# Attention over two key blocks in place of three with guards, a weight ring of 16 slots, and the first MLP products of two passes in seven-product form

## The chip, the cores and the metric

The kernel is one program that runs on all 8 cores of a Trainium2 chip, each core on two of the 16 sequences; the cores exchange nothing. The metric is the device time of the slowest core in microseconds. Engines are named PE (TensorE), DVE (VectorE), ACT (ScalarE), POOL (GpSimd) and SP (SyncE).

## The reference

```python
# x (16, 2048, 1024) float32; two layers; four MLP quarters of 1024 hidden columns each
for layer in range(2):
    xn = rmsnorm(h, mix_norm_g[layer])
    if layer == 0:
        p = xn @ ab_w_in                              # 2048 columns
        a_out = pool_mixer(p[:512]); b_out = gate_b * short_conv(gate_c * xb)
        mix = concat([a_out, b_out]) @ ab_w_out
    else:
        p = xn @ cd_w_in                              # 2560 columns: u, v, q, k, value
        c_out = spatial_gating(gelu(u), gelu(v))      # within 128-position chunks
        d_out = stick_breaking_attention(q, k, v)     # 8 heads of 64
        mix = concat([c_out, d_out]) @ cd_w_out
    h = h + mix
    hn = rmsnorm(h, mlp_norm_g[layer])
    h = h + square(relu(hn @ mlp_w1[layer])) @ mlp_w2[layer]
return rmsnorm(h, final_norm_g)

# attention: weight of key s for query t > s
#   A[t, s] = sigmoid(z_ts) * prod_{s<j<t} (1 - sigmoid(z_tj)),   z = q.k / 8
```

The reference sums over all earlier keys. The product in A falls fast with distance, so that only near keys count in float32.

## The kernel before

Each core holds its two sequences (s=0, 1) transposed, channels on partitions, and works through them in two halves of 1024 positions (p=0, 1), each half in two tiles (t=0, 1) of 512 positions. The residual stream `h` is float32 in on-chip memory; `xn` (normed input), `mix` and `hid` (hidden values of one MLP quarter) are bf16. A weight block of 128 output columns by 1024 inputs fills two slots of `ring` (12 slots, 6 blocks in flight). In p=0 the blocks come as float32 from `wblk` and are cast on the way, and SP stores them as bf16 in `wsc`, from where later passes load them.

`program` writes the stages in turn and weaves main work with side work: layer 0's input and mixers (`layer0_in`), `out_proj`, `mlp(s, l)` for layer l, layer 1's input (`layer1_in`), and `attention(s, p)`, which lies beside an MLP of the other sequence. The order on each engine is then set by a planner (`Sched.order`): from entered durations it works out a latest time for every operation and lists them by it, engine by engine. Every change of a duration or of the work therefore replans all stages.

The MLP has four quarters. A first product (`up`) is 8 matmuls of 128x128 weights by 512 columns for each of 8 blocks and 2 tiles; ACT applies Relu in the bank and Square into `hid`. The second product (`pairs`) adds to `h` on DVE. Where the sums of a pair of weight blocks exist in `wcm`, it runs in seven-product form (`strassen`): a group of two blocks by two tiles by two halves of the inputs takes 7 products of 4 matmuls, 28 in place of 32, with sums of the moving operand made by DVE (`tsum`). `combos` makes the weight sums (4 element-wise operations on 128x512) the first time that the blocks pass, on DVE for layer 0 and on POOL for layer 1, and SP stores them. `up_strassen` is the same form for the first product: it stands in the code but is called by nobody, since no call of `mlp` has `alone` or `mk` set.

The attention handles one unit for each of 4 pairs of heads, 16 query blocks of 128 and 2 sequences, 128 units in all. A unit scores its queries against the query's own block and the two before it (PE, L2134, two heads side by side in the rows of the array), ACT makes keep = sigmoid(-z/8), a DVE scan multiplies from the right (C, L2143), DVE subtracts neighbours (A), SP transposes A by DMA into AT, and PE multiplies with V (L2177, two heads side by side in the columns). POOL copies the leftmost product of each row to `flags`. If at the end one of them is over 0, a general kernel over all keys runs behind the first one.

## Time and profile before

| | |
|---|---|
| three runs | 2658.72, 2695.6, 3011.68 us; median 2695.6 |
| profiled execution | 2660.62 us, spans of the cores 2643.1 to 2659.0 |
| TensorE busy, slowest core | 2559.8 us (96%) |
| VectorE, ScalarE, GpSimd busy | 1555.2, 1119.1, 685.5 us |
| mean granted TensorE clock, by core | 0.991 to 0.994 |

The first row is what the comparison rests on; the others are of one execution and its slowest core, core 7. The chain that ended last goes through TensorE for 87% of the span. A line such as L1384 or L1397 is that of a helper that all stages use, so the tiles tell which stage a row belongs to: ps<-xn is a product from the normed input, ps<-hid and ps<-TT the second MLP product in seven-product form.

### The profile page before, as it was taken

Reading aid. Unit: us, or ns where it says so; the run is one execution under the profiler, and the core shown is the slowest. Engines: PE = TensorE matmul, PEld = TensorE weight load, DVE = VectorE, ACT = ScalarE, POOL = GpSimd, SP = SyncE. Lnnn points to the kernel's source line nnn. Section 1 sums busy time; section 2 is a strip of 40 time slices with the busy share of each in tenths; the row PEclk is TensorE's granted clock in tenths of the full one; section 3 lists DMA queues with packets and bytes.
Section 4 is the critical chain, followed back from the end, with each engine's and each line's share of the span. In section 5 each row is a group of like instructions: output and inputs, shape, how many; then the busy total and the mean of one; then the engine's idle time right before and its main releaser. Section 6 shows DMA issues by size and latency. Waiting matters only on the chain.

```text
span 2659.0 us, 38510 instructions; the slowest of 8 cores (2643.1 to 2659.0 us)
## 1 busy us (share of the span) xinstructions
PE 2559.8 (96%) x12392; PEld 1125.4 (42%) x12392; DVE 1555.2 (58%) x2133; ACT 1119.1 (42%) x1685; POOL 685.5 (26%) x1081
## 2 busy tenths in 40 slices
PE   5899999999999999999999999999999999999996
PEld 1344444444444444444444444444444443444443
DVE  2771337468674775436476533667776588854435
ACT  3335223464334642264333444236442364345432
POOL 2531111222112353621245211212322122311111
PEclk9999999999999999999999999999999999999998
DMA  6677884746454996855472233423564236533534
GB/s 137 152 151 159 185 188 114 160 109 140 125 125 109 166 199 131 206 159 168 124 223 79 72 101 102 135 72 93 129 136 131 76 85 133 117 103 111 161 113 148
DMA packets 237627, 354.05 MB, mean 133 GB/s; under 512 B 121072, under 2 KB 126576, under 8 KB 237424
## 3 DMA queue, kind: packets, MB, share of 16 engines
q0 software_dynamic: 77952, 227.92, 36.8%
q1 hardware_dynamic: 158896, 122.54, 18.0%
q8 instruction: 108, 1.77, 0.3%
q10 hardware_dynamic: 576, 1.05, 0.1%
q14 instruction: 95, 0.78, 0.1%
HBM read 298.26 MB, written 79.69 MB: 142 GB/s over the span
## 4 chain that ended last, share of the span: by engine, by line
PE 87%; DMA 4%; issue 3%; DVE 3%; POOL 2%; ACT 1%; SPq 0%; DVEq 0%; POOLq 0%; ACTq 0%
PE ps L1384 65%; PE ps L1498 19%; DMA ring<-wblk 2%; PE ps L2177 1%; PE ps L2134 1%; DMA ring<-wcm 1%; DMA h<-xT 1%; DVE xn L1400 1%; POOL X L1397 1%; POOL TT L1397 1%; ACT ps L1393 1%; DMA AT<-A 1%; DVE h L1397 0%; PE ps L2052 0%; SPq L1681 0%
## 5 line engine op out<-in xcount | busy, mean ns | idle before, releaser
L1384 PE MATMUL ps<-xn,ring 128*128 128x512 bf16 x5872 | 1312.0, 381 | 29.5 <-ACT XB L1393 7.7
L1384 PEld LDWEIGHTS ps<-xn,ring 128*128 128x128 bf16 x5872 | 564.9, 98 | 716.2 <-issue 60.2
L1397 DVE TENSOR_TENSOR h<-ps,h 128x512 f32<-128x512 f32 x816 | 552.3, 687 | 526.2 <-PE ps L1498 348.0
L1393 ACT ACTIVATE ps<-ps 128x512 f32<-128x512 f32 x632 | 366.7, 583 | 677.8 <-PE ps L1384 353.0
L1322 POOL DMA_DIRECT2D ring<-wsc x364 | 196.5, 540 | 733.1 <-PE ps L1384 483.3
L1498 PE MATMUL ps<-hid,ring 128*128 128x512 bf16 x1408 | 331.5, 380 | 9.5 <-DMA ring<-wcm 4.8
L1393 ACT ACTIVATE hid<-ps 128x512 bf16<-128x512 f32 x512 | 304.3, 598 | 40.2 <-ACT ps L1393 1.8
L1393 ACT ACTIVATE xn<-h 128x2048 bf16<-128x2048 f32 (+1 forms) x92 | 152.9, 1682 | 364.8 <-DVE h L1397 344.2
L1384 PE MATMUL ps<-hid,ring 128*128 128x512 bf16 x1280 | 281.2, 379 | 0.0
L1322 POOL DMA_DIRECT2D ring<-wcm x214 | 114.5, 536 | 574.6 <-PE ps L1384 283.4
L1498 PE MATMUL ps<-TT,ring 128*128 128x512 bf16 x1056 | 255.8, 380 | 5.7 <-ACT ps L1393 3.5
L1400 DVE SCALAR_TENSOR_TENSOR xn<-h,cfs,ms 128x512 bf16<-128x512 f32 x256 | 199.4, 824 | 87.7 <-ACT ms L1393 87.7
L1384 PE MATMUL ps<-mix,ring 128*128 128x512 bf16 x1024 | 227.0, 382 | 0.0
L1498 PEld LDWEIGHTS ps<-hid,ring 128*128 128x128 bf16 x1408 | 133.4, 98 | 176.8 <-issue 23.3
L2143 DVE TENSOR_TENSOR_SCAN C<-keep,cbs 128x768 f32<-128x768 f32 x112 | 198.4, 1773 | 13.7 <-DVE A L1397 4.8
L1322 POOL DMA_DIRECT2D ring<-wblk x188 | 101.2, 539 | 405.5 <-PE ps L1384 328.7
L1384 PEld LDWEIGHTS ps<-hid,ring 128*128 128x128 bf16 x1280 | 123.8, 98 | 149.1 <-issue 0.9
L1498 PEld LDWEIGHTS ps<-TT,ring 128*128 128x128 bf16 x1056 | 98.4, 98 | 138.0 <-issue 28.3
L1384 PEld LDWEIGHTS ps<-mix,ring 128*128 128x128 bf16 x1024 | 100.5, 98 | 122.6 <-issue 4.0
L1393 ACT ACTIVATE keep<-ps 128x768 f32<-128x768 f32 (+2 forms) x128 | 98.4, 769 | 80.6 <-DVE C L2143 51.9
L1397 DVE TENSOR_TENSOR A<-C 128x766 bf16<-128x766 f32 (+2 forms) x128 | 120.8, 944 | 17.6 <-DMA AT<-A 16.7
L1384 PE MATMUL ps<-ring,xn 128*128 128x512 bf16 x512 | 112.8, 379 | 1.0 <-DVE vnb L1405 0.8
(85 smaller groups left out, 1311.3 us busy)
## 6 DMA issues: line engine op xcount, KB each, us to landing
ring<-wsc POOLq DMA_DIRECT2D x364, 256.0 KB, 3.1
ring<-wblk POOLq DMA_DIRECT2D x188, 256.0 KB, 5.7
ring<-wcm POOLq DMA_DIRECT2D x66, 512.0 KB, 4.1
ring<-wcm POOLq DMA_DIRECT2D x88, 384.0 KB, 3.8
wsc<-ring SPq DMA_DIRECT2D x124, 256.0 KB, 4.3
h<-xT SPq DMA_DIRECT2D x64, 256.0 KB, 7.2
wcm<-TT SPq DMA_DIRECT2D x64, 256.0 KB, 5.1
oT<-stg SPq DMA_DIRECT2D x56, 256.0 KB, 4.2
```

Source lines behind the costliest of these rows:

```text
L1322: S.op("pool", (lambda out, sr: (lambda eng: eng.dma_start(out=out, in_=sr)))(out, src[:, a * 512:e * 512]), rd=rd, wr=[self.t_ring[x] for ...
L1384: ins = pe.matmul(out, lhsT=l, rhs=r, start=(i == 0), stop=(i == n - 1), **({"skip_group_check": True} if skip else {}))
L1393: return self.S.op("act", lambda e: e.activation(out=out, in_=in_, func=func, **kw), rd=rd, wr=wr, dur=0.17 + n * 0.00083, aset=aset)
L1397: return self.S.op(eng, lambda e: e.tensor_tensor(out=out, in0=a, in1=b, op=op), rd=rd, wr=wr, dur=dur)
L1400: return self.S.op(eng, lambda e: e.scalar_tensor_tensor(out=out, in0=a, scalar=sc, in1=b, op0=op0, op1=op1), rd=rd, wr=wr, dur=dur)
L1498: ins = pe.matmul(out, lhsT=l, rhs=r, start=start and i == 0, stop=(i == 3), skip_group_check=True)
L2134: ins = pe.matmul(self.bap(zb[hh])[:, lo:hi], lhsT=mx[hp, t, 4 + a, qb * 128:(qb + 1) * 128], rhs=src(hp), start=True, stop=True, skip_gro ...
L2143: S.op("dve", lambda e: e.tensor_tensor_scan(out=C[:, ::-1], data0=keep[:, ::-1], data1=floor[:, ::-1], initial=1.0, op0=ALU.mult, op1=ALU ...
L2177: ins = pe.matmul(self.bap(pb)[hh * 64:hh * 64 + 64, qb * 128:(qb + 1) * 128], lhsT=lt, rhs=self.AT[ai][:, hh * 3 + jj, :], start=(n == 0) ...
```

## The change

- The attention scores a query block against its own block and one before (256 columns in place of 384); Kh, Vh, keep, C, A and AT shrink by a third or a half, and the DMA transpose moves 4 blocks in place of 6.
- Three guards replace the old one: the leftmost product must not exceed 2^-70 (`CTAIL`); the smallest square of an attention output, kept in `om` by an ACT square and a DVE minimum on each 128x512 output, not fall below 2^-76; and a bound on the column norms of the value weights (`vbound`) not exceed 3.9.
- The ring has 16 slots, 8 blocks. The loads of x for sequence 1 move two chunks each.
- `mlp(0, 0)` and `mlp(1, 1)` get `alone=True`: where `wcm` holds the sums of a quarter's first blocks, `up_strassen` is used, with the sums of xn made by `up_sums` in mix. `mk="dve"` makes those weight sums in p=0, in `mlp(1, 0)` for layer 0's blocks and in `mlp(1, 1)` for layer 1's. They did not exist before. The sums of the second product stay on the engines that they were on.
- `up_strassen` itself changes: the third product (c) goes to bank 4 alone and is copied by ACT to a float32 tile cT; DVE adds bank b and cT into bank d (0 or 1) or into cT; product a has bank 5.

```diff
-RING = 12
+RING = 16
 NAT = 5
 OUTS = False
 MM8 = 1.735
+CTAIL = 2.0 ** -70
+OFLOOR = 2.0 ** -76
+VCEIL = 3.9
...
-        self.Kh = new("Kh", [128, 4, 256], BF16)[0]
-        self.Vh = new("Vh", [128, 2, 512], BF16)[0]
+        self.Kh = new("Kh", [128, 4, 128], BF16)[0]
+        self.Vh = new("Vh", [128, 512], BF16)[0]
...
+        self.cT = [new("cT%d" % i, [128, 512], F32, at=mx[0][1] + 12288 + i * 2048)[0] for i in range(2)]
...
-            def add(dst, a, b):
-                x, y = st[a], st[b]
-                o = self.tt("dve", self.bap(st[dst]), self.bap(x), self.bap(y), ALU.add,
-                            [self.t_bank[x], self.t_bank[y]], [self.t_bank[st[dst]]], 0.69)
+            def add(out, tout):
+                x, i = st["b"], st["i"]
+                self.tt("dve", out, self.bap(x), self.cT[i][:], ALU.add, [self.t_bank[x]] + tm[1][4 + 2 * i:6 + 2 * i], tout, 0.69)
 
             def p1():
                 st["pos"] = self.take((2, b, 0))
                 i = self.rr.get("su", 0) % 2
                 self.rr["su"] = i + 1
...
-                st["a"], st["c"], st["b"], st["d"] = 0, (1, 4)[i], 2 + i, 5
+                st["i"], st["a"], st["c"], st["b"], st["d"] = i, 5, 4, 2 + i, i
                 prod("a", 0, lambda i: X[:, 0, i, :], tX[0][0:4], True)
                 self.act(self.bap(st["b"]), self.bap(st["a"]), AF.Copy, [self.t_bank[st["a"]]], [self.t_bank[st["b"]]], 470)
 
             def p5():
                 prod("c", 2, lambda i: m[:, 0, i, :], tm[0][0:4], True)
+                i = st["i"]
+                self.act(self.cT[i][:], self.bap(st["c"]), AF.Copy, [self.t_bank[st["c"]]], tm[1][4 + 2 * i:6 + 2 * i], 490)
...
             def p6():
                 prod("b", 3, lambda i: m[:, 0, 4 + i, :], tm[0][4:8], False)
-                add("d", "b", "c")
+                add(self.bap(st["d"]), [self.t_bank[st["d"]]])
...
             def p7():
                 prod("b", 5, lambda i: X[:, 1, i, :], tX[1][0:4], False)
-                add("c", "b", "c")
-                bi = st["c"]
-                self.stt(hd[:, 1, j2, :], self.bap(bi), 0.0, self.bap(bi), ALU.max, ALU.mult, [self.t_bank[bi]], [td[1][j2]])
+                i = st["i"]
+                tc = tm[1][4 + 2 * i:6 + 2 * i]
+                add(self.cT[i][:], tc)
+                self.stt(hd[:, 1, j2, :], self.cT[i][:], 0.0, self.cT[i][:], ALU.max, ALU.mult, tc, [td[1][j2]], dur=0.72)
...
+        w = 1 if s == 0 else 2
         for t in tiles:
-            for c in range(8):
-                src = self.xT[s, c * 128:(c + 1) * 128, p * 1024 + t * 512:p * 1024 + (t + 1) * 512]
-                self.S.op("sp", (lambda t, c, src: (lambda e: e.dma_start(out=self.h[s][:, t, c, :], in_=src)))(t, c, src),
-                          rd=list(after), wr=[self.t_h[s][t][c]], dur=0.45, dma=("h", s, t, c), nbytes=262144)
+            for c in range(0, 8, w):
+                src = self.xT[s, c * 128:(c + w) * 128, p * 1024 + t * 512:p * 1024 + (t + 1) * 512].rearrange(
+                    "(a p) n -> p a n", a=w)
...
+                        if which == 1 and s == 0 and p == 0:
+                            self.vbound(slots)
...
+            self.act(TT[:, k, :], self.rs(slots[k]), AF.Square, [self.rt(slots[k])], [self.t_TT[k // 4][k % 4 // 2]], 512)
+        bi = self.bank("n")
+        self.mms(self.bap(bi), [(self.ones[:], TT[:, k, :]) for k in range(8)],
+                 self.t_TT[0] + self.t_TT[1] + [self.t_ones], [self.t_bank[bi]], MM8)
...
-                blocks = [gi - 2 + jj for jj in range(3)]
+                blocks = [gi - 1, gi]
                 segs = []
                 nh = sum(1 for b in blocks if 0 <= b < p * 8)
                 if nh:
-                    b0 = max(0, gi - 2) - (p * 8 - 2)
-                    segs.append((c0, c0 + nh * 128, lambda hp: self.Kh[hp, a, b0 * 128:(b0 + nh) * 128]))
-                m0 = max(p * 8, gi - 2) - p * 8
+                    segs.append((0, 128, lambda hp: self.Kh[hp, a, :]))
...
                     self.cp("dve", mx[:, t, 4 + a, :], self.bap(pb), [self.t_bank[pb]], [tm[t][4 + a]], 0.69)
+                    q0 = 256 if gi < 8 and t == 0 else 0
+                    k = a % 2
+                    sq = self.sq[s][k]
+                    self.act(sq[:, q0:512], mx[:, t, 4 + a, q0:512], AF.Square, [tm[t][4 + a]], [self.t_sq[k]], 512)
+                    self.tt("dve", self.om[:, q0:512], self.om[:, q0:512], sq[:, q0:512], ALU.min, [self.t_sq[k], self.t_om],
+                            [self.t_om], 0.43)
...
-            self.weave(sum(self.mlp(0, 0), []), [])
+            self.weave(sum(self.mlp(0, 0, alone=True), []), [])
...
-            self.weave(sum(self.mlp(1, 0), []), self.attention(0, p), upto=0.75)
+            self.weave(sum(self.mlp(1, 0, mk=None if p else "dve"), []), self.attention(0, p), upto=0.75)
...
-            self.weave(sum(self.mlp(1, 1, 3), []), side)
+            self.weave(sum(self.mlp(1, 1, 3, alone=True, mk=None if p else "dve"), []), side)
...
+        self.ts("dve", f[:, 4:5], f[:, 0:1], CTAIL, None, ALU.is_gt, None, [t2], [t2], 0.1)
+        self.ts("dve", f[:, 5:6], f[:, 1:2], OFLOOR, None, ALU.is_lt, None, [t1], [t1], 0.1)
+        self.ts("dve", f[:, 6:7], f[:, 2:3], VCEIL, None, ALU.is_gt, None, [self.t_vs], [self.t_vs], 0.1)
+        self.tt("dve", f[:, 4:5], f[:, 4:5], f[:, 5:6], ALU.max, [t1, t2], [t2], 0.1)
+        self.tt("dve", self.fl3[:, 0:1], f[:, 4:5], f[:, 6:7], ALU.max, [t2, self.t_vs], [t3], 0.1)
```

Instructions in the fast part of the program, before and after: PE 12398 and 12038; 128x512 matmuls from xn and ring 5888 and 5376, from mix and ring 1024 and 1408; value matmuls 720 and 496; DVE operations TT from ring 64 more, TT from TT and ring and the reverse 64 more together; DMA stores to wcm 128 and 256.

**PE at the start of mlp(0,0) of the second half.** Before: xn_46 is sequence 1 (layer 0's input), pb the pool mixer's products, xn_45 sequence 0, whose MLP begins.

```order
L1384 MATMUL ps<-xn_46,ring 128x512 x80
L1384 MATMUL ps<-pb,cbs 128x512 x2
L1384 MATMUL ps<-xn_45,ring 128x512 x16
L1384 MATMUL ps<-pb,cbs 128x512 x2
L1384 MATMUL ps<-xn_45,ring 128x512 x240
L1498 MATMUL ps<-hid_47,ring 128x512 x4
L1498 MATMUL ps<-TT,ring 128x512 x8
```

After:

```order
L1394 MATMUL ps<-xn_46,ring 128x512 x64
L1394 MATMUL ps<-pb,cbs 128x512 x4
L1588 MATMUL ps<-xn_45,ring 128x512 x4
L1588 MATMUL ps<-mix_49,ring 128x512 x4
L1588 MATMUL ps<-xn_45,ring 128x512 x4
L1588 MATMUL ps<-mix_49,ring 128x512 x8
L1588 MATMUL ps<-xn_45,ring 128x512 x12
L1588 MATMUL ps<-mix_49,ring 128x512 x4
L1588 MATMUL ps<-xn_45,ring 128x512 x4
```

The 256 matmuls of two quarters in plain form become groups of four over xn, mix (the sums of xn) and again xn, and both pool products now stand ahead of the first of them.

**DVE at the same place.** Before: xn_45 is scaled by the norm (ms), pb closes the pool mixer, mix_50<-ps,Y the convolution of sequence 1.

```order
L1400 SCALAR_TENSOR_TENSOR Y<-PR,cfs,Y 128x1024
L1400 SCALAR_TENSOR_TENSOR xn_45<-h_43,cfs,ms_61 128x512
L1397 TENSOR_TENSOR mix_50<-ps,Y 128x512
L1400 SCALAR_TENSOR_TENSOR pb<-X_82,PA 128x1024
L1400 SCALAR_TENSOR_TENSOR xn_45<-h_43,cfs,ms_61 128x512 x2
L1397 TENSOR_TENSOR mix_50<-ps,Y 128x512
L1397 TENSOR_TENSOR TT<-hid_47 128x2048
```

After:

```order
L1407 TENSOR_TENSOR mix_49<-xn_45 128x2048
L1410 SCALAR_TENSOR_TENSOR xn_45<-h_43,cfs,ms_61 128x512 x3
L1410 SCALAR_TENSOR_TENSOR pb<-X_85,PA 128x1024
L1410 SCALAR_TENSOR_TENSOR xn_45<-h_43,cfs,ms_61 128x512
L1410 SCALAR_TENSOR_TENSOR Y<-PR,cfs,Y 128x1024
L1407 TENSOR_TENSOR mix_49<-xn_45,mix_49 128x1024 x2
L1407 TENSOR_TENSOR mix_50<-ps,Y 128x512 x2
L1407 TENSOR_TENSOR xn_45<-xn_45 128x1024
L1407 TENSOR_TENSOR ps<-ps,cT_77 128x512
L1407 TENSOR_TENSOR xn_45<-xn_45 128x1024
```

Two mix_49<-xn_45,mix_49 of 1024 elements stand between Y and mix_50<-ps,Y, the sum of 2048 elements ahead of them; the rest of the sums and the first sum of a group (ps,cT) follow.

**PE in the first attention**, woven with sequence 1's MLP (xn_46). Before, K,mix are scores and AT,V value products.

```order
L2134 MATMUL ps<-K,mix_49 128x384 x2
L2177 MATMUL ps<-AT_70,V 64x128 x6
L1384 MATMUL ps<-xn_46,ring 128x512 x8
L2134 MATMUL ps<-K,mix_49 128x384 x2
L1384 MATMUL ps<-xn_46,ring 128x512 x16
L2177 MATMUL ps<-AT_71,V 64x128 x6
L1384 MATMUL ps<-xn_46,ring 128x512 x8
```

After:

```order
L2168 MATMUL ps<-K,mix_49 128x256 x2
L2211 MATMUL ps<-AT_73,V 64x128 x4
L1394 MATMUL ps<-xn_46,ring 128x512 x16
L2168 MATMUL ps<-K,mix_49 128x256 x2
L1394 MATMUL ps<-xn_46,ring 128x512 x8
L2211 MATMUL ps<-AT_74,V 64x128 x4
L1394 MATMUL ps<-xn_46,ring 128x512 x16
```

The scores lose 128 columns, the value products two of six matmuls; the number of groups between MLP matmuls is the same.

## Rows read from the trace of the kernel before

**Rows 1.** The page's header and its busy times by engine.

```profile
span 2659.0 us, 38510 instructions; the slowest of 8 cores (2643.1 to 2659.0 us)
...
PE 2559.8 (96%) x12392; PEld 1125.4 (42%) x12392; DVE 1555.2 (58%) x2133; ACT 1119.1 (42%) x1685; POOL 685.5 (26%) x1081
```

**Rows 2.** Stretches: length, busy us of PE, PEld, DVE, ACT, POOL, clock, DMA share, GB/s.

```profile
105.00:2640.00 2535.00, 2491.07 (x12125) 1098.23 (x12122) 1496.75 (x2052) 1079.68 (x1637) 647.84 (x1027) 1.00 0.55 132
513.00:755.00 242.00, 240.53 (x1256) 103.02 (x1255) 168.87 (x217) 116.59 (x188) 51.26 (x96) 1.00 0.52 124
1485.00:1511.00 26.00, 23.71 (x109) 10.28 (x107) 25.88 (x28) 9.65 (x16) 10.27 (x11) 1.00 0.23 66
1508.00:1720.00 212.00, 209.95 (x965) 93.51 (x966) 87.81 (x130) 90.41 (x149) 37.51 (x70) 1.00 0.37 110
```

**Rows 3.** Pieces of the chain that ended last: start, us, what.

```profile
1030.95 161.55 PE ps L1384 x748
...
1565.12 21.98 PE ps L1498 x100
```

**Rows 4.** TensorE in order of time, 560 to 600 us: start, us, group.

```profile
560.18 0.34 PE L2134 MATMUL ps<-K,mix 64*128 64x384 bf16 x2
560.45 0.36 PE L2177 MATMUL ps<-AT,V 128*64 128x128 bf16 x6
560.74 1.90 PE L1384 MATMUL ps<-xn,ring 128*128 128x512 bf16 x8
562.57 0.34 PE L2134 MATMUL ps<-K,mix 64*128 64x384 bf16 x2
...
580.58 0.30 PE L2177 MATMUL ps<-AT,V 128*64 128x128 bf16 x4
580.81 3.63 PE L1384 MATMUL ps<-xn,ring 128*128 128x512 bf16 x16
...
587.62 0.28 PE L2134 MATMUL ps<-K,mix 64*128 64x256 bf16 x2
587.84 1.90 PE L1498 MATMUL ps<-hid,ring 128*128 128x512 bf16 x8
```

**Rows 5.** Groups by line and form: busy us, mean ns, idle before them.

```profile
L1397 DVE TENSOR_TENSOR h<-ps,h 128x512 f32<-128x512 f32 x816 | 552.3, 687 | 526.2 <-PE ps L1498 348.0 <-PE ps L1384 170.8 <-DVE h L1397 0.3
L1393 ACT ACTIVATE ps<-ps 128x512 f32<-128x512 f32 x632 | 366.7, 583 | 677.8 <-PE ps L1384 353.0 <-PE ps L1498 316.7 <-DVE A L1397 4.3
...
L1393 ACT ACTIVATE hid<-ps 128x512 bf16<-128x512 f32 x512 | 304.3, 598 | 40.2 <-ACT ps L1393 1.8
...
L2143 DVE TENSOR_TENSOR_SCAN C<-keep,cbs 128x768 f32<-128x768 f32 x112 | 198.4, 1773 | 13.7 <-DVE A L1397 4.8 <-POOL flags L1409 3.9 <-ACT keep L1393 3.4
...
L1397 DVE TENSOR_TENSOR A<-C 128x766 bf16<-128x766 f32 x112 | 110.8, 990 | 5.4 <-DMA AT<-A 5.0 <-DVE C L2143 0.2
...
L1397 DVE TENSOR_TENSOR TT<-hid,TT 128x1024 bf16<-128x1024 bf16 x88 | 58.1, 682 | 36.7 <-ACT hid L1393 36.6
...
L1397 DVE TENSOR_TENSOR TT<-hid 128x2048 bf16<-128x2048 bf16 x22 | 26.7, 1213 | 19.4 <-ACT hid L1393 19.3 <-issue 0.2
...
L1397 DVE TENSOR_TENSOR TT<-ring 128x512 bf16<-128x512 bf16 x32 | 13.5, 423 | 124.8 <-DMA ring<-wblk 123.9
```

**Rows 6.** Waits of TensorE, 105 to 2640 us: total, times, longest.

```profile
PE ps L2177 <- DMA AT<-A: 5.6, 2, 4.5
...
PE ps L1498 <- DMA ring<-wcm: 4.8, 5, 2.2
PE ps L1384 <- DVE st L2026: 4.7, 2, 2.4
```

**Rows 7.** TensorE in order of time, in front of mlp(0,0) of the second half.

```profile
1508.70 1.89 PE L1384 MATMUL ps<-xn,ring 128*128 128x512 bf16 x8 [1.38 <-DVE mix L1397]
```

**Rows 8.** Two stretches of 20 us (columns as in rows 2).

```profile
820.00:840.00 20.00, 17.50 (x85) 7.87 (x84) 12.51 (x33) 10.83 (x15) 6.09 (x11) 1.00 0.15 41
840.00:860.00 20.00, 20.00 (x93) 8.85 (x92) 10.07 (x16) 8.88 (x13) 5.40 (x10) 0.91 0.75 162
```

101 lines of the change are left out of this document (63 added, 38 removed).

## The prediction

> **What bounds the kernel now.** I read the page's header and busy shares first, then stretches of the middle, the gaps of TensorE by releaser, and last the spacing of its instructions. TensorE is busy 2559.8 of 2659.0 us and nothing else comes near it: VectorE, the next, has 1555.2 us [rows 1]. From 105 to 2640 us, without the start and the last norm, TensorE is busy 2491.07 of 2535 us [rows 2], so all waits of the middle are 44 us. It is a kernel that shortens by what leaves TensorE's queue, provided no new wait appears. The profiled execution took 2660.6 us, 1.6 us more than its span. The median of the three runs is 2695.6 us, 1.3% above it, with a lowest of 2658.7. I sum against the profiled one, and I expect a comparable run of the changed kernel to come out near that sum.
>
> **TensorE's real prices.** The mean of one matmul (about 380 ns on the page) is a latency. The price is the distance between starts: 748 matmuls of 512 columns took 161.55 us, 0.216 each [rows 3]. In the attention I take the start of a group to the start of the next [rows 4]: two score matmuls of 384 columns 560.18 to 560.45, 0.27 us; two of 256 columns 587.62 to 587.84, 0.22; six value matmuls 560.45 to 560.74, 0.29; four 580.58 to 580.81, 0.23. So a pair of value matmuls is worth 0.06 us, since the two heads use different halves of the array.
>
> **1. Two key blocks in place of three.** Of the 128 units, the 112 from the third query block of a sequence on lose a block: 224 value matmuls (720 become 496), 112 times 0.06 is 6.7 us. Scores: 96 of them go from 384 to 256 columns at 0.05 us, 4.8 us. The 16 at the start of the second half also lose part or all of the read from Kh: the 8 first units go from 256 plus 128 to 128 plus 128 columns (0.05 each), and the 8 second units from two pairs of matmuls to one, about 0.17 each (an estimate, 0.22 less the 0.05 that 128 columns are worth). That is 1.8 us, and 6.6 for the scores. Sum: **13.3 us**. The units still switch TensorE between kinds of matmul: eight matmuls between a score group and the next score group take 1.83 us, 560.74 to 562.57 [rows 4], where eight times 0.216 are 1.73. That 0.10 per switch stays, for there are as many groups as before.
>
> The Trainium skill (TensorEngine Tiling (Array Packing), Key Properties) says that changing the tiling mode drains TensorE. By that rule the trace agrees, with the 0.10 us. The same page, under Instruction Overhead, gives each matmul some 60 cycles of overhead; charging all 224 one by one at the estimate of 60 cycles of 2.4 GHz more than their 128 columns would make their saving 17 us in place of 6.7, and the forecast 2615.
>
> VectorE and ScalarE also get lighter: a scan of 768 elements takes 1.77 us and a subtraction of 766 0.99 [rows 5]; a third less of both is 0.92 us, an estimate that leaves out what is fixed in each, so 112 times at most 0.92, 103 us of VectorE. Directly it is worth nothing, since VectorE isn't what ends. What it and the smaller transpose can remove are the waits on them: 5.6 us of TensorE behind AT<-A and part of the 4.7 behind a statistics step of VectorE [rows 6]. I take 5 us, between 0 and 10.
>
> **2. The guards.** 32 squares on ScalarE (0.598 each by hid<-ps of the same shape [rows 5]), 32 minima on VectorE (0.42 by TT<-ring [rows 5]), 14 us of VectorE in four attentions, hidden. The bound on V adds eight 512-column matmuls, 1.7 us. Should a guard fire, the general kernel would run behind this one. That doesn't depend on time but on numbers, so I evaluated the reference on its own inputs: the largest product over two blocks is 2^-86 against the limit 2^-70, the smallest output past the first two blocks 7e-8 in size against 2^-38 (3.6e-12), and the bound on V 1.21 against 3.9. I hold the fallback at 1 in 100 (roundings, or an order that leaves a flag unwritten).
>
> **3. Seven products for the first MLP products.** `wcm` has sums for blocks 24 and 108 only after the first half (p=0) has made them, so the form runs in two passes of the second half: mlp(0,0) and mlp(1,1). Each has 4 quarters of 4 groups, and a group goes from 32 to 28 matmuls: 32 groups by 4 is 128 matmuls, by 0.216 **27.6 us**. The order shows just that: 512 fewer from xn, 384 more from mix. Less the 1.7 us of part 2, TensorE's queue loses 27.6 + 13.3 - 1.7 = **39.2 us**.
>
> What a group asks of the others: TensorE 28 by 0.216, 6.05 us. ScalarE two copies and three pairs of Relu and Square, 2 by 0.583 and 3 by 1.181 [rows 5], 4.71 us, as much as the four pairs of before (4.72) but in a shorter group. VectorE two sums of 0.69 [rows 5] and one product, about 2.1 us. No engine is full, so what matters is the return trip: the third product waits for ScalarE's copy of the first, the fifth for VectorE's sum. The nearest row is the second MLP product, which has this form already with one such copy: a group there starts every 6.17 us (100 matmuls in 21.98 us [rows 3], against 21.6 at 0.216), 0.12 lost per group. Here there are two copies and Relu pairs in the same ScalarE queue, one bank (5) for product a and one (4) for product c. Bounds: 0 and the 1.3 us that ScalarE has to spare. I take 0.2 by 32, 6 us, near the existing row.
>
> **The seam** in front of mlp(0,0). The sums of xn (one of 2048 and, six times, of 1024 elements, at 1.21 and 0.68 us [rows 5], 5.3 us) land in the place where VectorE is busy 25.88 of 26 us and TensorE already loses 2.3 [rows 2]; it waits there 1.38 us for mix<-ps,Y [rows 7]. VectorE's order now puts three of them ahead of those two mix<-ps,Y, and TensorE finishes all four pool products before the MLP instead of running 16 matmuls of it between them. Bounds 0 and 6; I take 3. In front of mlp(1,1) the norm is long done, so 0.
>
> **4. The weight sums** for these passes: 32 pairs by 4 operations at 0.423 [rows 5], 54 us of VectorE and 128 more DMA stores on SP's queue, all in the first half. Half of it lies beside the attention from 513 to 755 us, where VectorE is busy 168.9 of 242 [rows 2] and gets 27 more and up to 29 less by part 1; it cancels. SP's queue holds transposes behind stores that wait for VectorE; the ring of 16 (8 blocks in flight, not 6) covers later releases. I take 0, with 5 as the upper end. GpSimd keeps the sums that it has (TT on POOL is unchanged in the order). Merged loads of x for the second sequence: 0. The deeper ring: 4.8 us of TensorE's waits are on ring<-wcm [rows 6], 1 of which I count. It may also pull weight loads into the start; 0, within 3 either way.
>
> **Sum:** 2659.0 - 39.2 - 5 - 1 + 6 + 3 = 2623, and with 1.6 outside the span **2625 us**, 1.3% less. What a measurement of this kernel can tell from no change is about 2%, here 53 us: the forecast lies inside.
>
> **Rivals.**
> *All cover holds* (chance 0.17). No wait in the groups or at the seam, all 10 us of attention waits gone, and a fall of the clock avoided: after the 2.4 us gap in 820 to 840 the granted clock was 0.91 in the next 20 us [rows 8], worth about 1.8. 2659 - 39 - 10 - 5 - 2 gives 2603 and 2605 us in all. For it: TensorE at 240.5 of 242 in an attention woven with much work. Against: nothing lets more than the waits go.
>
> *The return trip binds* (0.14). Each seven-product group loses 1.2 us: product a must be free of Square before the next first product, and ScalarE's queue also holds the final norm's squares in mlp(1,1). 32 by 1.2 is 38 us: 2659 - 39 - 6 + 38 + 3, **2657 us**. For it: single banks for a and c. Against: the 0.12 us of the present form.
>
> *Slower* (0.05). The same place, one price higher: if a whole round of ScalarE's eight operations (4.7 us) stood open in every group, because the copy is queued behind the last group's pairs, the 32 groups would cost 32 by 3.2 us or more and the span pass 2659 + 60; it decides from 2.9 us a group on. About 2720 us. Bank 2/3 alternating and the order (copy ahead of the pairs) speak against it.
>
> The Trainium skill (TensorE: Matmul & The Clock Gate, A second HAM failure mode) describes a kernel in which short idles between groups that cycle through PSUM banks bring the clock down again and again. In this kernel that would sit in the same 32 groups. As a mechanism in rows: the one fall above cost 1.8 us, and one in each of the 8 quarters 14 us, 2639 us in all. The stretches of the middle show 1.00, groups of this kind inside [rows 2], so I give it 0.03.
>
> *It doesn't do what it says* (0.02 with the fallback): the form would not run, 27.6 us stay, 2643 us; the order excludes it. A fallback would be thousands of us.
>
> **Chances and range.** Forecast 0.59 (2610 to 2645), the rivals as above. The bounds of the unknown costs are 39 + 12 below and nearly 0 net above. The range 2598 to 2668 holds all but the slower rival and some of the tails. Faster by over 2% means below 2607: most of the first rival, 0.14. Slower by over 2% is above 2714: 0.06. Within 2%: 0.80.
>
> **What would show it.** TensorE's instructions fall by 360. Score pairs at 0.22 us and value groups of four at 0.23 confirm part 1. From the first seven-product matmul to the last, starts 0.216 apart with gaps of a few tenths behind ScalarE confirm part 3; idle of more than 1 us per group behind ps or cT shows the return trip. Waits of TensorE behind AT<-A near 0, and the seam's wait under 6 us. I'd be wrong if the planner's new order opens a wait in a stage that I haven't looked at, for all stages were planned anew, or if the start (the first 105 us) moves by more than 3 us.

## The result and the profile after

The changed kernel's profiled execution took 2625.01 us, span 2623.4, where 2625.0 were predicted. Against the kernel before its time has the ratio 0.9864 (95% interval 0.9822 to 0.9907): 1.4% less, which is inside the 2% that this measurement can tell from no change. Comparisons leave disturbed executions out; e8 and e9 have too few others for an interval and are compared by their profiled execution. A second measurement of the changed kernel (e12) gave 0.9874 (0.9850 to 0.9898).

The header and the busy times of the page after, beside [rows 1]:

```profile
span 2623.4 us, 38836 instructions; the slowest of 8 cores (2605.8 to 2623.4 us)
...
PE 2523.5 (96%) x12032; PEld 1106.3 (42%) x12032; DVE 1626.0 (62%) x2405; ACT 1109.8 (42%) x1725; POOL 658.4 (25%) x1088
...
DMA packets 225105, 386.52 MB, mean 147 GB/s; under 512 B 91104, under 2 KB 100448, under 8 KB 224896
```

TensorE lost 360 instructions and stayed at 96%; VectorE went up by 71 us. Stretches of the kernel after, columns as in [rows 2]:

```profile
105.00:2610.00 2505.00, 2460.12 (x11793) 1081.67 (x11793) 1568.43 (x2335) 1073.89 (x1681) 621.42 (x1035) 1.00 0.57 147
513.00:755.00 242.00, 240.03 (x1223) 103.06 (x1221) 177.72 (x292) 113.91 (x197) 51.81 (x103) 1.00 0.67 179
1485.00:1511.00 26.00, 20.77 (x87) 8.48 (x86) 26.00 (x30) 8.99 (x14) 10.55 (x9) 0.90 0.17 51
1080.00:1130.00 50.00, 44.75 (x199) 19.72 (x198) 17.30 (x28) 3.82 (x2) 31.41 (x35) 0.93 0.88 227
1130.00:1300.00 170.00, 169.34 (x781) 75.98 (x780) 103.10 (x180) 93.94 (x151) 27.30 (x50) 1.00 0.72 229
1540.00:1720.00 180.00, 179.01 (x820) 78.76 (x819) 111.27 (x164) 70.79 (x115) 38.17 (x70) 1.00 0.47 147
```

The first attention is as full as before (240.03 of 242). The seam (1485 to 1511) lost 2.9 us more than in [rows 2] and fell to a clock of 0.90. New is a hole of 5.3 us in 1080 to 1130. TensorE in order of time (start, us, group) in the attention, in seven-product groups, at the seam and at that hole, to be held against [rows 4] and [rows 7]:

```profile
547.42 0.28 PE L2168 MATMUL ps<-K,mix 64*128 64x256 bf16 x2
547.63 0.30 PE L2211 MATMUL ps<-AT,V 128*64 128x128 bf16 x4
547.87 1.90 PE L1394 MATMUL ps<-xn,ring 128*128 128x512 bf16 x8
...
1125.96 9.39 PE L1394 MATMUL ps<-hid,ring 128*128 128x512 bf16 x33 [5.25 <-DVE h L1407]
...
1506.71 1.01 PE L1394 MATMUL ps<-pb,cbs 128*128 128x512 bf16 x2 [3.44 <-DVE pb L1410]
1508.33 1.87 PE L1588 MATMUL ps<-xn,ring 128*128 128x512 bf16 x4 [0.61 <-ACT mix L1403]
...
1542.43 1.89 PE L1588 MATMUL ps<-mix,ring 128*128 128x512 bf16 x8
1544.16 1.03 PE L1588 MATMUL ps<-xn,ring 128*128 128x512 bf16 x4
1545.02 1.03 PE L1588 MATMUL ps<-mix,ring 128*128 128x512 bf16 x4
1545.88 2.75 PE L1588 MATMUL ps<-xn,ring 128*128 128x512 bf16 x12
1548.72 1.89 PE L1588 MATMUL ps<-mix,ring 128*128 128x512 bf16 x8
```

A score pair now takes 0.21 (547.42 to 547.63) and a value group 0.24, together the 0.45 that was predicted. A seven-product group starts 6.29 us after the last (1542.43 to 1548.72), 0.24 over 28 times 0.216. The waits of TensorE (total, times, longest), beside [rows 6], and groups by form, beside [rows 5]:

```profile
PE ps L1394 <- DVE PR L1407: 5.8, 5, 2.1
PE ps L1394 <- DVE h L1407: 5.3, 1, 5.3
PE ps L1394 <- DVE st L2043: 4.6, 2, 2.3
PE ps L1394 <- DVE pb L1410: 4.0, 3, 3.4
...
PE ps L1588 <- ACT ps L1403: 2.2, 4, 0.8
PE ps L1588 <- DMA ring<-wcm: 1.9, 2, 1.3
...
PE ps L2211 <- DMA AT<-A: 1.1, 1, 1.1
```

```profile
L1407 DVE TENSOR_TENSOR h<-ps,h 128x512 f32<-128x512 f32 x816 | 554.9, 688 | 336.3 <-PE ps L1394 172.9 <-PE ps L1508 154.9 <-issue 0.5
...
L2177 DVE TENSOR_TENSOR_SCAN C<-keep,cbs 128x512 f32<-128x512 f32 x120 | 152.6, 1272 | 18.1 <-ACT keep L1403 8.4 <-DVE A L1407 6.3 <-POOL flags L1419 2.1
...
L1407 DVE TENSOR_TENSOR A<-C 128x510 bf16<-128x510 f32 x120 | 85.9, 716 | 8.0 <-DMA AT<-A 7.4 <-DVE C L2177 0.5
...
L1407 DVE TENSOR_TENSOR TT<-ring 128x512 bf16<-128x512 bf16 x96 | 39.8, 420 | 144.5 <-DMA ring<-wblk 105.5 <-DMA ring<-wsc 36.5
```

A scan and a subtraction are 0.50 and 0.27 us shorter, the wait on AT fell from 5.6 to 1.1, and the statistics step stayed. The second products (L1498 before, L1508 after) no longer wait for ring<-wcm, 4.8 before; the 1.9 in the rows is a new wait, of the seven-product first products (L1588). What stands behind the wait of 5.25 us is in VectorE's row at that time (in brackets its own wait), and in GpSimd's, which issues the weight loads:

```profile
1113.91 0.69 DVE L1407 TENSOR_TENSOR h<-ps,h 128x512 f32<-128x512 f32 x1 [1.03 <-PE ps L1394]
1124.19 0.43 DVE L1407 TENSOR_TENSOR TT<-ring 128x512 bf16<-128x512 bf16 x1 [9.59 <-DMA ring<-wsc]
1124.79 0.42 DVE L1407 TENSOR_TENSOR TT<-TT,ring 128x512 bf16<-128x512 bf16 x1 [0.17 <-DVE TT L1407]
1125.13 0.68 DVE L1407 TENSOR_TENSOR h<-ps,h 128x512 f32<-128x512 f32 x1
```

```profile
1119.60 1.15 POOL L1407 TENSOR_TENSOR TT<-TT,ring 128x512 bf16<-128x512 bf16 x1 [0.20 <-POOL TT L1407]
1120.69 0.56 POOL L1332 DMA_DIRECT2D ring<-wsc  x1
```

VectorE had reached the first weight sum of mlp(1,1), whose block wasn't there; the load was issued at 1120.69, behind GpSimd's own sums. The addition to h behind it, at 1125.13, was the one that TensorE's bank waited for. This wait isn't one core's: it is TensorE's longest in 1080 to 1380 us on all eight cores, 2.9 to 8.3 us.

**A common measure.** The slowest core isn't the same one from run to run, and planned orders differ, so stage ends don't compare directly. I therefore worked out a **loss** from the traces: the distance from each matmul's start to the next one's, less its price (0.216 for 512 columns, 0.06 plus 0.02 per 100 columns for a score matmul, 0.11 per value group plus 0.03 per matmul), summed over a stretch. It holds waits, slow clock and switches; what is left of the span is the **work**: the matmuls at these prices, and what follows the last matmul (a median of 18.6 us before, 17.9 in the changed kernel, 20.0 in e1, 20.7 in e2). So the work counts matmuls and does not test the prices; a wrong price would show as loss. Medians in us over the six cores whose traces have all matmuls (cores 2 and 4 lack some 240). "start" ends with the first half's pool products, "after" is all behind it; of that, "att.1" is from the first V to the second, "att.2" from the second V to the second half's pool products (attention and mlp(1,1)), "0,0" the pool products and mlp(0,0) of the second half, "end" what follows the last V:

```
kernel                        span    work   start  after    att.1  att.2   0,0    end
before                       2650.5  2528.5   51.2   72.2      8.9   17.4   12.0   19.8
changed                      2616.3  2488.2   55.8   73.3      7.9   16.5   20.6   20.0
e1 plain first products      2619.9  2518.3   50.9   51.1      5.9    9.5   13.3   13.3
e2 sums made, not used       2634.6  2518.7   53.3   62.1      7.8   16.8   13.3   14.9
e3 ring of 12                2622.4  2488.3   51.6   81.2      7.3   18.0   24.8   20.4
e4 sums behind products      2625.4  2488.5   48.3   87.9     14.1   24.7   21.0   19.7
e5 form alone                2652.7  2501.2   54.4   99.4     12.1   25.7   22.3   23.8
e6 ring 12, single loads     2629.7  2489.1   49.9   91.1      7.3   23.8   23.8   24.5
e7 no guards                 2624.0  2487.6   55.0   82.2      7.5   21.3   20.8   21.7
e8 GpSimd, all of mlp(1,1)   2617.4  2488.1   54.5   73.6      7.0   17.7   19.9   22.4
e9 plain, ring of 12         2637.5  2516.7   56.1   63.5      7.0   15.1   14.1   16.1
e10 first pass only          2622.5  2505.2   56.0   61.3      8.0    8.7   20.1   13.5
e11 GpSimd, first quarter    2619.3  2488.0   55.3   75.5      8.0   17.8   20.9   20.4
```

The work fell by 40.3 us, about 1 of it behind the last matmul, where 39.2 were predicted. The start scatters from 48 to 56 with no relation to what was changed, so the losses after it are compared. Within one execution "after" spreads by 3 (e10) to 21 us (e11) over the cores, most of it in att.2; most other stages agree within 3.

Each row is one execution. All executions that the ratios rest on have these spans, start included, by the median of eight cores: changed 2617.1 to 2621.6 (with e12), e1 2619.9 to 2625.6 (the row above is the lowest), e2 2631.3 to 2634.3, e3 2625.9 to 2633.1, e9 2637.5 and 2640.9, e10 2617.6 to 2622.5. A term of 2 or 3 us from two rows is therefore not told from this scatter; those of 7 us and more are.

### The profile page after: what moved, and what is told of

Read it like the earlier page. It is cut to its first block, busy times and chain, and to the rows that moved or that the text cites. A ratio compares the mean times of both kernels' runs of the same rounds, so it can differ in the third digit from the quotient of the medians.

```text
span 2623.4 us, 38836 instructions; the slowest of 8 cores (2605.8 to 2623.4 us)
## 1 busy us (share of the span) xinstructions
PE 2523.5 (96%) x12032; PEld 1106.3 (42%) x12032; DVE 1626.0 (62%) x2405; ACT 1109.8 (42%) x1725; POOL 658.4 (25%) x1088
## 2 busy tenths in 40 slices
DMA packets 225105, 386.52 MB, mean 147 GB/s; under 512 B 91104, under 2 KB 100448, under 8 KB 224896
## 4 chain that ended last, share of the span: by engine, by line
PE 86%; DMA 5%; issue 3%; DVE 3%; ACT 1%; POOL 1%; SPq 0%; DVEq 0%; POOLq 0%; ACTq 0%
PE ps L1394 56%; PE ps L1508 20%; PE ps L1588 7%; DMA h<-xT 2%; DMA ring<-wblk 2%; PE ps L2211 1%; PE ps L2168 1%; DVE xn L1410 1%; POOL X L1407 1%; DMA ring<-wcm 0%; SPq L1696 0%; DVE stg L1410 0%; DVE Y L1410 0%; ACT ps L1403 0%; POOL TT L1407 0%
## 5 line engine op out<-in xcount | busy, mean ns | idle before, releaser
L1394 PE MATMUL ps<-xn,ring 128*128 128x512 bf16 x4848 | 1093.6, 382 | 33.5 <-DVE PR L1407 10.2
L1394 PEld LDWEIGHTS ps<-xn,ring 128*128 128x128 bf16 x4848 | 464.0, 98 | 595.6 <-issue 57.6
L1508 PE MATMUL ps<-hid,ring 128*128 128x512 bf16 x1408 | 327.2, 379 | 0.6 <-DVE h L1407 0.2
L1332 POOL DMA_DIRECT2D ring<-wcm x277 | 149.3, 539 | 705.8 <-PE ps L1508 282.8
L1332 POOL DMA_DIRECT2D ring<-wsc x300 | 162.8, 543 | 554.2 <-PE ps L1394 350.8
L1403 ACT ACTIVATE hid<-ps 128x512 bf16<-128x512 f32 x480 | 284.6, 597 | 34.2 <-ACT ps L1403 1.1
L1508 PE MATMUL ps<-TT,ring 128*128 128x512 bf16 x1056 | 254.1, 379 | 1.9 <-ACT ps L1403 1.3
L1410 DVE SCALAR_TENSOR_TENSOR xn<-h,cfs,ms 128x512 bf16<-128x512 f32 x256 | 208.2, 857 | 56.0 <-ACT ms L1403 56.0
L1508 PEld LDWEIGHTS ps<-hid,ring 128*128 128x128 bf16 x1408 | 134.8, 98 | 163.8 <-issue 3.7
L2177 DVE TENSOR_TENSOR_SCAN C<-keep,cbs 128x512 f32<-128x512 f32 x120 | 152.6, 1272 | 18.1 <-ACT keep L1403 8.4
L1508 PEld LDWEIGHTS ps<-TT,ring 128*128 128x128 bf16 x1056 | 99.0, 97 | 130.5 <-issue 18.4
L1407 DVE TENSOR_TENSOR TT<-ring 128x512 bf16<-128x512 bf16 x96 | 39.8, 420 | 144.5 <-DMA ring<-wblk 105.5
L1588 PE MATMUL ps<-xn,ring 128*128 128x512 bf16 x512 | 123.2, 382 | 1.2 <-ACT mix L1403 0.6
```

Source lines behind the costliest of these rows:

```text
L1332: S.op("pool", (lambda out, sr: (lambda eng: eng.dma_start(out=out, in_=sr)))(out, src[:, a * 512:e * 512]), rd=rd, wr=[self.t_ring[x] for ...
L1394: ins = pe.matmul(out, lhsT=l, rhs=r, start=(i == 0), stop=(i == n - 1), **({"skip_group_check": True} if skip else {}))
L1403: return self.S.op("act", lambda e: e.activation(out=out, in_=in_, func=func, **kw), rd=rd, wr=wr, dur=0.17 + n * 0.00083, aset=aset)
L1407: return self.S.op(eng, lambda e: e.tensor_tensor(out=out, in0=a, in1=b, op=op), rd=rd, wr=wr, dur=dur)
L1410: return self.S.op(eng, lambda e: e.scalar_tensor_tensor(out=out, in0=a, scalar=sc, in1=b, op0=op0, op1=op1), rd=rd, wr=wr, dur=dur)
L1508: ins = pe.matmul(out, lhsT=l, rhs=r, start=start and i == 0, stop=(i == 3), skip_group_check=True)
```

## Experiments

**e1: plain first products.** All calls back to `mlp(0, 0)`, `mlp(1, 0)`, `mlp(1, 1, 3)`: no form, no sums for it.

```diff
-            self.weave(sum(self.mlp(0, 0, alone=True), []), [])
+            self.weave(sum(self.mlp(0, 0), []), [])
-            self.weave(sum(self.mlp(1, 0, mk=None if p else "dve"), []), self.attention(0, p), upto=0.75)
+            self.weave(sum(self.mlp(1, 0), []), self.attention(0, p), upto=0.75)
-            self.weave(sum(self.mlp(1, 1, 3, alone=True, mk=None if p else "dve"), []), side)
+            self.weave(sum(self.mlp(1, 1, 3), []), side)
```

> The changed kernel with the first MLP products of all passes in plain form: no sums of their weights are made and no seven-product groups run. Attention over two blocks, guards and ring of 16 stay. My sum gives the form 27.6 us less 0.24 us a group (8 us, groups start every 6.29 us in the trace after), less the seam (about 3) and less the wait of 5.3 us behind a VectorE sum at 1120 us with its fall of the clock (about 7 in all): 2623 plus 10, a span of about 2633 us. Rival, the form is worth its full 27.6 us and the wait at 1120 has another cause: 2651 us.

Measured: 0.9907 (0.9873 to 0.9941). The whole form, 27.6 us of matmuls, is worth 0.3 to 0.4%, with intervals that overlap those of the changed kernel. The loss after the start is 22.2 us lower than in the changed kernel, and 21.1 lower than before.

**e2: the weight sums are made and stored, but not used.** `mk` stays, `alone` goes from both calls.

> The changed kernel with the weight sums made and stored in the first half as before, and the seven-product form not used: what the sums alone cost, against e1. If they cost only the wait at 1120 us, e2 is 5 to 7 us above e1 (about 2640 us) and shows a wait of TensorE behind DVE h of some 5 us there, which e1 doesn't. Rival, the sums are hidden: e2 equals e1 within 2 us.

Measured: 0.9947 (0.9929 to 0.9964). This splits the 22.2: the sums alone cost 11.0 us of loss (62.1 against 51.1; 1.9 of it in att.1, 7.3 in att.2), the form itself 11.2 (73.3 against 62.1). The wait for h is there on all eight cores, 3.3 to 7.9 us, as on the slowest:

```profile
PE ps L1394 <- DVE h L1407: 5.6, 1, 5.6
```

In e1 TensorE's longest wait for h there is 0.8 us on any core.

**e3: a ring of 12** (`RING = 12`).

> The changed kernel with 12 slots of the ring in place of 16. If the ring of 16 is what brings more weight loads into the start (58.6 us of TensorE in the first 100 us against 63.6 before), the start comes back by 3 to 5 us; against that the waits on ring<-wcm and the supply around 1080 to 1125 us get worse by some us. Net 2618 to 2630 us. Rival, the depth does nothing for the start, which is then due to the merged loads of x: first 100 us as in the changed kernel, 2625 to 2632 us.

Measured: 0.9945 (0.9926 to 0.9964); loss after the start 81.2, 7.9 more than with 16. The times of the slowest cores say more: a median of 2640.4 us against 2624.9 and, in e12, 2628.5.

**e4: the sums behind the products.** The first and the last of the four operations of `combos` also wait for the last hid of their pair (the two between follow the first), so that the planner puts them later.

```diff
-                            self.combos(base + q * 16 + j - 1, hold[0], hold[1], mk)
+                            self.combos(base + q * 16 + j - 1, hold[0], hold[1], mk, [td[1][j]])
```

> The changed kernel, where each weight sum of the first products waits also for the hidden value that the same pair of blocks makes last, so that VectorE never stands before a weight load that TensorE does not need yet. If the sum of weights in VectorE's queue is the cause, the 5.3 us wait behind DVE h at 1120 us and the clock of 0.83 there go: 7 us less, a span of about 2616 us. Rival, the supply of the ring is the bound there and TensorE then waits for ring<-wblk itself: 2621 to 2625 us.

Measured: 0.9936 (0.9917 to 0.9955), slower than the changed kernel. The wait at 1126 went, but TensorE's waits (e4's slowest core) are now led by ones that the changed kernel has at 1.3 and 0.2 us:

```profile
PE ps L1509 <- ACT ps L1403: 10.1, 11, 2.0
PE ps L1509 <- DVE h L1407: 5.3, 10, 1.2
```

I read this as the sums running into the second products, whose additions and sums of hid stand in the same queue. My theory, that only the order of this one operation was at fault, fell.

**e5: the form alone**, in the kernel before: the new `up_strassen`, cT, `alone` and `mk`, with three key blocks, ring of 12, old guard.

> The kernel before (three key blocks, ring of 12, single loads, one guard) with nothing but the seven-product form of the two passes and its weight sums by VectorE. Theory A, from the accounts of the first runs: TensorE's queue loses 27.6 us, the groups give back 7.6, seam and second pass 4, the handover of the weight sums 9, so 7 us remain or less: ratio to the kernel before 0.997 to 1.000, span about 2652 to 2659, and because VectorE is fuller in the attention here (scans of 1.77 us) the sums in the first attention may cost more than the 2.1 us that they cost with two blocks. Rival B: what the form is worth (18.6 us by my prediction) is there, and it was the other parts that gave less: ratio 0.993, span about 2641. The stage from V2 to the pool products of the second half should be 7 to 9 us longer than before by A.

Measured: 1.001 (0.9979 to 1.0041), theory A, though the ratio lies just above its 0.997 to 1.000 and the stage from V2 to the pool products is 6.3 us longer than before (548.3 against 542.0) where A said 7 to 9. The loss rose by 27.2 us (99.4 against 72.2) and ate the 27.6. Waits in att.2, slowest core:

```profile
PE ps L1385 <- DVE h L1398: 7.8, 1, 7.8
PE ps L2180 <- DMA AT<-A: 5.9, 3, 4.5
```

The wait on AT of [rows 6] stays with three blocks, beside the new wait for h.

**e6: ring of 12 and single loads of x** (`w = 1`).

> The changed kernel with a ring of 12 and the loads of x for sequence 1 again one chunk each. It stands beside e3, ring of 12 with loads of two chunks (span 2638.7, pool products of the first half done at 205.3 us, TensorE busy 58 us of the first 100; the kernel before 200.7 and 64). Theory A: the merged loads cost the start 3 to 5 us, since a norm step can't begin until both chunks are there: here TensorE is busy 62 us or more of the first 100, the pool products end at 202 or before, and the span is 3 to 5 us under that of e3. Rival B: the start was lost to the new order of the queues: 205 us again, the span within 1.5 us of e3.

Measured: 0.992 (0.9899 to 0.9941). The slowest core did what theory A says (TensorE busy 65.28 us of the first 100, pool products done at 199.6), but over all eight cores the pool products end at a median of 199.9 us against 200.6 in e3, and the start's loss is 49.9 against 51.6. The slowest core of a run is often the one with the worst start, so reading the start there was a choice of the sample. Neither theory has its numbers: A's shorter span didn't come (2643.0 against 2638.7), and B's 205 us in the slowest core didn't either. What the eight cores show is nearer to B: the merged loads cost the start 2 us or less, and the span isn't shorter without them.

**e7: no guards.** The square and minimum at `if qb == 3` and the call of `vbound` are taken out, with their part of `flag`.

> The changed kernel without two of its guards (it leaves out the squares and minima of the attention's outputs and the bound on the value weights; the check on the leftmost product stays). Theory A: only the eight matmuls of the bound are on TensorE's path, 1.7 us, and 14 us of VectorE and 19 of ScalarE lay hidden: span 1 to 3 us under that of the changed kernel, 2621. Rival B: the minima stand in VectorE's queue in front of steps that TensorE waits for: 5 us or more, 2617 or less, and shorter attention stages.

Measured: 0.9881 (0.9863 to 0.9898), not faster than the changed kernel (0.9864, 0.9874). The stretch up to the first V is 1.7 us shorter (245.6 against 247.3), the eight matmuls of the bound, as predicted; att.1 is alike (7.5 and 7.9), so squares and minima are hidden. Att.2, which spreads widely over the cores, has 21.3 here against 16.5; no guard is in the changed kernel's wait there, and I take it for that spread, which isn't shown.

**e8: GpSimd makes the sums of mlp(1,1)** (`mk=None if p else "pool"` there).

> The changed kernel with the weight sums of mlp(1,1) made by GpSimd in place of VectorE; those of mlp(1,0) stay on VectorE. Theory A: the loss of 7 us in mlp(1,1) of the first half is VectorE's in-order queue standing at a sum whose weight block is still in flight, with additions to h behind it that free TensorE's banks: on GpSimd nobody stands behind it, the wait of TensorE for h near 1126 us (5.25 us) and the low clock behind it go, the stretch from V2's end (840.3) to the pool products (1379.0) becomes 5 to 8 us shorter, span about 2616 to 2618. Rival B: GpSimd is slower (an operation takes over 1 us in place of 0.42) and has the sums of the second products already, ring slots are held longer and TensorE waits for weights instead: span 2623 or more, with waits on ring.

Measured: median span 2617.4 (slowest core 2632.2), att.2 17.7 against 16.5: no gain. From 1085 to 1150 us TensorE has 65.00 (twice 64.68) of 65 us on the eight cores; the wait that theory A names is gone. But behind it time is lost on most of them, as on core 2:

```profile
1080.00:1150.00 70.00, 69.63 (x320) 31.69 (x325) 29.28 (x35) 26.90 (x38) 53.24 (x56) 1.00 0.82 219
1150.00:1180.00 30.00, 19.46 (x86) 8.57 (x87) 5.12 (x4) 13.72 (x24) 18.21 (x19) 0.83 0.97 276
```

Neither theory as written: TensorE waited up to 10.3 us (core 2) for ScalarE's hid, and for ring<-wsc up to 2.3, on three cores only.

**e9: plain, ring of 12.**

> The changed kernel in plain form (no weight sums for it, no seven-product form in the first products, as e1) and with a ring of 12: attention over two blocks, guards and merged loads alone. By medians of the eight cores e1 (ring of 16) had 2619.9 us, the kernel before 2650.5, and with the form the ring of 12 cost 8.9 us (e3 2625.9 against 2617.0), where my prediction gave the ring 1 us. Theory A: the ring is worth 7 to 9 us without the form too, since it covers the weight loads in the woven stages: median span here 2627 to 2630, and the attention is worth about 22. Rival B: the ring is needed only because the form holds blocks longer: here within 2 us of e1, 2618 to 2622, and the attention is worth about 30. The second attention's stage (V2's end to the pool products, 529.0 in e1, 542.0 before) tells whether the 13 us won there are the ring's or the attention's.

Measured: loss after the start 63.5, 12.4 more than e1's; the ring is worth what theory A says, and more. The median span, 2637.5, is above A's 2627 to 2630, so the attention (with guards and merged loads) is worth 13.0 us of span here and not 22; 4.9 us of the gap is the start. The loss after it is 8.7 less than in the kernel before. The stage that the expectation names takes 534.4 us, against 529.0 in e1 and 542.0 before: 5 us are the ring's, 8 the attention's. The third attention, from the first V to the next first V, is the stage where cores agree best. It takes 334.8 us before, 329.1 in e3 and 329.4 here, and 327.4 with the ring of 16. Stretch 1130 to 1300 us in core 0 of e9, with its largest wait in the second attention and mlp(1,1), and in core 6 of e1:

```profile
PE ps L1508 <- DMA ring<-wcm: 5.1, 2, 3.0
...
1130.00:1300.00 170.00, 164.41 (x757) 1.00 0.50 146
```

```profile
1130.00:1300.00 170.00, 169.66 (x785) 76.40 (x784) 81.79 (x123) 90.52 (x150) 28.48 (x52) 1.00 0.49 152
```

(e9's row: TensorE only.) Core 3 of e9 lost 6.6 us once behind AT<-A. With the ring of 16 such waits for weights are mostly gone: in att.2 seven of e1's eight cores have none over 1 us, one has 1.9.

**e10: first pass only.** `alone` and `mk` go from mlp(1,1).

> The changed kernel with the form and its weight sums only in mlp(1,0) and mlp(0,0); mlp(1,1) is plain in both halves. Theory A: by stages, the second pass costs 9 us (V2's end to the pool products 538.0 against 529.0 in e1) and brings 9 (end stage 503.6 against 513.0): median span 2617 within 2, as the changed kernel, with 529 in the first of these stages and 513 in the last. Rival B: part of the 9 us is knock-on of the sums in mlp(1,0) (other DMA traffic, an order planned anew), so it stays 4 us or more above 529 here, and the median span is 2620 or more.

Measured: 0.9872 (0.9853 to 0.9892). Theory A in the stage: att.2 loses 8.7, as e1's 9.5, and takes 529.5 us. The span, 2622.5, is B's and not A's 2617: by medians of the eight cores, beside the changed kernel, 2.8 us lie before the pool products of the first half and 2.9 behind the last matmul (20.8 against 17.9, and 20.0 in e1), where A had counted nothing. The first pass nets 13.8 less 10.2 (61.3 against 51.1), 3.6 us; the second 13.8 less 12.0, 1.8.

**e11: GpSimd for the first quarter of mlp(1,1) only.**

```diff
-                            self.combos(base + q * 16 + j - 1, hold[0], hold[1], mk)
+                            self.combos(base + q * 16 + j - 1, hold[0], hold[1], "pool" if l == 1 and q == 0 else mk)
```

> The changed kernel with one thing moved: the weight sums of the first quarter of mlp(1,1) (4 pairs, 16 operations) are GpSimd's, the other quarters' and those of mlp(1,0) stay VectorE's. In e8 GpSimd's sums left TensorE full from 1085 to 1150 us on every core and lost 0 to 10 us from 1150 on, where the second quarter's sums met those of the second products; in the changed kernel VectorE's lost 3 to 9 us from 1110 to 1130 and next to nothing behind. Theory A (a sum at the head of VectorE's in-order queue, in front of an addition to h that frees a bank, is the whole loss, and only while the second products of the last MLP still run): both losses go, the stage is 529 to 532 us in place of 538.0, median span 2609 to 2612, ratio to the kernel before 0.983 to 0.985. Rival B (the loss is the added DMA traffic, 8 MB more of stores in this stage, whoever makes the sums): the stage stays at 536 or above and the waits move to ring or to the second quarter.

Measured: 0.9892 (0.9872 to 0.9913), att.2 17.8; rival B in its outcome. TensorE is again full to 1150 us, and five cores then lose 7.5 to 10.7 us in one wait. Core 2, ScalarE and TensorE in order of time:

```profile
1163.76 0.60 ACT L1403 ACTIVATE hid<-ps 128x512 bf16<-128x512 f32 x1
1176.92 1.91 ACT L1403 ACTIVATE xn<-h 128x2048 bf16<-128x2048 f32 x1 [12.56 <-DMA oT<-stg]
```

```profile
1180.57 7.22 PE L1394 MATMUL ps<-xn,ring 128*128 128x512 bf16 x24 [10.67 <-ACT hid L1403]
```

and the stretches there in core 2 and in core 1, which lost nothing (clock, DMA share and GB/s are the last three):

```profile
1150.00:1160.00 10.00, 9.95 (x47) 4.51 (x46) 3.31 (x8) 6.81 (x12) 1.75 (x4) 1.00 0.99 309
1160.00:1170.00 10.00, 9.85 (x45) 4.31 (x44) 3.72 (x8) 3.17 (x6) 0.55 (x1) 1.00 1.01 297
1170.00:1180.00 10.00, 0.00 (x0) 0.00 (x0) 1.62 (x5) 3.08 (x4) 0.54 (x1) 0.71 1.04 316
```

```profile
1150.00:1160.00 10.00, 10.00 (x48) 4.53 (x47) 4.73 (x10) 6.83 (x12) 0.54 (x1) 1.00 1.06 375
1160.00:1170.00 10.00, 10.00 (x49) 4.49 (x47) 0.00 (x0) 8.48 (x13) 1.09 (x2) 1.00 1.04 303
1170.00:1180.00 10.00, 9.72 (x46) 4.28 (x45) 8.86 (x13) 7.70 (x13) 1.09 (x2) 1.00 0.55 157
```

The DMA engines are full for 20 to 30 us: final outputs go out (oT), x of the second half comes in (h<-xT, issued from 1100 to 1180 us, took a median of 12.7 us in core 2, 5.7 in core 5 of e1), weights come in and the sums go out. ScalarE stands 12.56 us at the first squares of the new x, with the Relus that free TensorE's banks behind them. The row names a store of a final output as what came last, at 1176.57; a load of x beside it on the same queue landed at 1176.90, so which of them held ScalarE isn't settled, and both had been under way for 15 us. Core 1 moved 375 GB/s at the worst moment and was through 10 us earlier; it had also begun 10 us earlier:

```profile
1140.00:1150.00 10.00, 10.00 (x48) 4.58 (x47) 6.30 (x13) 6.74 (x12) 1.78 (x4) 1.00 1.02 305
```

```profile
1140.00:1150.00 10.00, 9.95 (x47) 4.56 (x47) 3.36 (x8) 6.72 (x13) 7.16 (x9) 1.00 0.80 218
```

(core 1, then core 2). From 1140 to 1180 us both moved 11.4 MB, so core 2's burst was later and not smaller. The pattern is that of 1126 us in the changed kernel, on another engine: an in-order queue stands at an operation that waits for a transfer. The Trainium skill (Perfetto Trace Analysis, Engine Utilization) gives 358 GB/s as a core's share of memory when both cores of a pair draw on it. The full stretches here are of that order, 297 to 316 in core 2 and 303 to 375 in core 1, one of them above that figure; no run here loaded one core alone.

**e12: the changed kernel again.**

> The changed kernel itself once more, beside e9 to e11 on one chip: how far its own number moves between chips. Median span of the cores 2615 to 2621, ratio 0.986 to 0.988; stage from V2's end to the pool products 536 to 541 us, spread over the cores 8 to 10 us.

Measured: 0.9874 (0.9850 to 0.9898); cores 0 to 3 span 2615.5 to 2622.5 us, and in them the stage att.2 takes 537.5 to 539.1 us, where the first execution has a median of 538.0 (533.0 to 543.2 over its cores). The wait for h is there again, 4.4 to 7.8 us.

## Why the prediction was right, and what in it was not

The time and the verdict came out as forecast, within 2% and 1.4% below. By its own steps:

- **TensorE's queue, -39.2:** -40.3 of work, of which about -1 lies behind the last matmul. The count is in the trace (360 fewer); the prices are tested apart from it: 0.21 and 0.24 for a score pair and a value group where 0.22 and 0.23 were taken, and 1.7 us for the bound (e7).
- **Waits that the lighter attention gives back, -5 (0 to -10):** -8.7 (e9 against before, with guards and merged loads in it), inside the bounds. In the third attention 5.4 us went (334.8 to 329.4); by the prediction's prices its 32 units make 4.0 of them.
- **The deeper ring, -1:** this term was mis-sized. It is worth 12.4 us of loss without the form (e1 against e9) and 7.9 with it (changed against e3). I had priced it by the 4.8 us that TensorE waits for ring<-wcm in one core of one execution; those waits are gone (L1508 has none there), and the rest of the gain lies in waits that this row doesn't name; which ones wasn't shown.
- **Groups and seam, +9:** 11.2 (changed against e2). A group is 0.24 over its price where 0.2 was taken, 7.7 us in 32; the seam in front of mlp(0,0) is 3.5 (7.3 more in "0,0" than e2, less 16 by 0.24), where 3 was taken, nearly all in the wait for pb. (The row of the form that was there gives 6.15 us a group and 0.11 lost, where the prediction read 6.17 and 0.12; its term of 0.2 doesn't hang on that.)
- **The weight sums, 0 (up to 5):** the other mis-sized term. They cost 11.0 us (e2 against e1), over their upper end of 5. The prediction's step counted VectorE's busy time beside the first attention and let it cancel against the shorter scans. That stretch indeed costs only 1.9; 7.3 are in att.2, in mlp(1,1), where I hadn't looked: VectorE isn't short of time there, it stands in order at a block still in flight. The step had named the stores on SP's queue, not their traffic: by the pages of the profile 42 MB more than in e1 (386.52 against 344.53), which is 32 pairs by 0.917 MB stored and 0.393 MB more loaded each.
- **Start, 0 (3 either way):** +4.6 between the two executions, over the 3 and inside a scatter of 8. So both things that the prediction said would prove it wrong did happen: the start moved by more than 3 us, and the new order opened a wait in a stage that hadn't been looked at (5.25 us at 1126).
- **The rivals.** The return trip doesn't bind: 0.24 per group, and the seven-product stretch 1540 to 1720 runs at 179.01 of 180 us. The fall of clock in every quarter did not come either: the granted clock is 1.00 over that stretch, with 0.24 us lost per group. The Trainium skill (TensorE: Matmul & The Clock Gate, A second HAM failure mode) tells of a kernel in which short idles between groups bring the clock down again and again; the trace here doesn't show it. The means below 1.00 above (0.93 in 1080 to 1130, 0.90 at the seam) are stretches spent in part at the lower level, 1.2 GHz, behind the waits of 5.25 and 3.44 us.

The measured terms, -40.3 - 8.7 - 12.4 + 11.2 + 11.0 + 4.6, give -34.6; the median spans differ by 34.2 and the slowest cores by 35.6. That they add up is no test, since each is a difference between two rows of one table. The mechanism of the forecast, fewer matmuls in a full queue, holds, but that the time came out at 2625.0 to the microsecond is luck: two errors of about 11 us cancel, and without the ring's extra the time would have been about 2636, without the sums' cost about 2614.

**What stays open.** That VectorE stands at a weight sum in mlp(1,1), with TensorE's bank behind it, is shown: the wait is on all eight cores with VectorE's sums (changed, e2), and gone without them (e1) or with GpSimd making them (e8, e11). That the added traffic is what makes mlp(1,1) lose time, whichever engine makes the sums, is argued from the full DMA engines in e8 and e11; a kernel that makes the sums and doesn't store them wasn't run. No version tried beats the changed kernel: e7 (0.9881) and e10 (0.9872) lie within its interval, with less code.
